# Merge stage: the mLSTM branch by Strassen pairs, the attention branch in plain tiles one pair ahead, the modulation's gate sums moved into the projections

## What is computed

```python
u = rmsnorm(x, norm_pre_w) * (1 + scale) + shift
aq, ak, av, az, mq, mk, mv, mo, mz, mg, ga, gb = split_proj(u, w_in)
y_b = attention(aq, ak, av) * silu(az)                      # (T, 1024)
y_a, C, n, m = mlstm_branch(mq, mk, mv, mo, mz, mg, ...)    # (T, 1024)
merged = sigmoid(ga) * (y_a @ w_proj_a) + sigmoid(gb) * (y_b @ w_proj_b)   # (T, 2048)
out = rmsnorm(merged @ w_out, norm_post_w)
return x + gate * out
```

## Time and profile before

| | |
|---|---|
| median of three runs | 1955.51 us (1955.37 to 1955.70) |
| the profiled execution | 1955.12 us, span 1953.5 us |
| PE busy | 1920.3 us, 98% |
| DVE, ACT, POOL busy | 62%, 34%, 6% |
| mean granted PE clock | 0.998 |
| bytes moved | 274 MB, 140 GB/s in the mean |

### The profile page before, as it was taken

How to read it: one execution, slowest core, us unless ns; L and a number is a source line. 1 busy time by engine, 2 the same in 40 slices (tenths; PEclk the granted TensorE clock), 3 DMA queues, 4 the chain that set the end, 5 groups by cost and what they waited for, 6 DMA issues and landing times.

```text
span 1953.5 us, 31682 instructions
## 1 busy us (share of the span) xinstructions
PE 1920.3 (98%) x12266; PEld 1782.6 (91%) x12266; DVE 1204.0 (62%) x2073; ACT 668.8 (34%) x1017; POOL 113.2 (6%) x201
## 2 busy tenths in 40 slices
PE   6999999999999999999999999999999999999998
PEld 2589999999999999999898999889889999988886
DVE  3368766666666666665766664465557767683224
ACT  4453333333333333332555554233224222242221
POOL 2010000000000000000000000000002000000000
PEclk9999999999999999999999999999999999999999
DMA  9962353333333333334632423355355666633224
GB/s 369 391 197 86 111 164 110 111 112 113 113 113 113 113 113 113 113 113 127 183 109 80 122 75 118 91 150 135 108 130 144 203 203 184 210 116 140 80 76 162
DMA packets 302319, 274.04 MB, mean 140 GB/s; under 512 B 20384, under 2 KB 253608, under 8 KB 300320
## 3 DMA queue, kind: packets, MB, share of 16 engines
q1 hardware_dynamic: 287984, 216.71, 37.9%
q0 software_dynamic: 13952, 56.00, 7.9%
q10 hardware_dynamic: 304, 0.25, 0.0%
HBM read 235.05 MB, written 40.48 MB: 141 GB/s over the span
## 4 chain that ended last, share of the span: by engine, by line
PE 91%; DVE 3%; DMA 3%; ACT 1%; issue 1%; SPq 1%; POOL 0%; DVEq 0%; POOLq 0%; ACTq 0%
PE bank L2060 20%; PE bank L2140 12%; PE bank L2133 12%; PE bank L2134 12%; PE bank L2356 11%; PE bank L2069 10%; PE bank L1973 2%; PE bank L2033 2%; PE bank L2260 2%; PE bank L2249 1%; PE bank L2201 1%; PE bank L2262 1%; PE bank L2178 1%; PE bank L2009 1%; DMA WORK<-in_w_ada_dram 1%
## 5 line engine op out<-in xcount | busy, mean ns | idle before, releaser
L2060 PE MATMUL bank<-XH,WH 128*128 128x320 f32 x1472 | 345.5, 316 | 2.8 <-DVE XL L1847 2.1
L1041 ACT ACTIVATE WH<-RAW 128x1024 fp32r<-128x1024 f32 x195 | 206.7, 1060 | 386.1 <-PE bank L2140 306.2
L2060 PE MATMUL bank<-XL,WH 128*128 128x320 f32 x1472 | 335.1, 309 | 0.0
L1482 DVE TENSOR_TENSOR WL<-RAW,WH 128x1024 fp32r<-128x1024 f32 x195 | 238.3, 1222 | 143.8 <-ACT WH L1041 143.8
L920 ACT ACTIVATE WH<-RAW 128x1024 fp32r<-128x1024 f32 x122 | 129.1, 1059 | 532.3 <-PE bank L2069 407.8
L2060 PEld LDWEIGHTS bank<-XH,WH 128*128 128x128 f32 x1472 | 244.5, 188 | 10.8 <-issue 8.0
L2060 PEld LDWEIGHTS bank<-XL,WH 128*128 128x128 f32 x1472 | 246.2, 188 | 0.0
L2069 PE MATMUL bank<-XH,WL 128*128 128x320 f32 x1472 | 235.9, 310 | 0.0
L2069 PEld LDWEIGHTS bank<-XH,WL 128*128 128x128 f32 x1472 | 220.0, 188 | 4.1 <-issue 3.8
L2134 PE MATMUL bank<-XL,WH 128*128 128x320 f32 x720 | 212.5, 309 | 0.0
L2133 PE MATMUL bank<-XH,WH 128*128 128x320 f32 x720 | 212.5, 309 | 0.0
(11 more groups left out here) (245 smaller groups left out, 2962.9 us busy)
## 6 DMA issues: line engine op xcount, KB each, us to landing
RAW<-in_w_in_dram SPq DMA_DIRECT2D x165, 512.0 KB, 3.8
WORK<-in_w_ada_dram SPq DMA_DIRECT2D x62, 512.0 KB, 5.4
proj_dram<-OUTS POOLq DMA_DIRECT2D x92, 320.0 KB, 2.5
RAW<-in_w_out_dram SPq DMA_DIRECT2D x32, 512.0 KB, 3.9
WORK<-proj_dram SPq DMA_DIRECT2D x16, 640.0 KB, 4.5
WORK<-proj_dram POOLq DMA_DIRECT2D x32, 320.0 KB, 3.3
RAW<-in_w_ada_dram SPq DMA_DIRECT2D x18, 512.0 KB, 9.3
RAW<-in_w_proj_a_dram SPq DMA_DIRECT2D x16, 512.0 KB, 4.7
```

The lines of the kernel that those rows point to most:

```text
L1041: ins = nc.scalar.activation(WH[:, (j + p) % 2, :], pair_raw(j, p), ACT.Copy)
L1482: V.tensor_tensor(WL[:, w, :], pair_raw(j, p), WH[:, w, :].bitcast(F32), ALU.subtract)\
L2060: pe.matmul(banks[n][:, 0:HALF_TOK], wh[:, k, :], x[:, k0 + k, n * HALF_TOK:(n + 1) * HALF_TOK], start=(first and k == 0 and wi == 0), sto ...
```

## The change

- **Merge, attention branch (B):** sixteen plain tiles `b_product(j)`, one half each (48 products). They use blocks 0 to 7 of XH and XL, which now hold attention's result (`shift` of `high_y` and `low_y`). `b_gate(j)` multiplies the banks by the sigmoids in place (MTB). Tiles 0 to 3 come first, then two after each mLSTM pair, one after pairs 5 and 6, none after 7 (`b_tiles`).
- **Merge, mLSTM branch (A):** eight Strassen pairs `a_product(i, p)`, p from 0 to 6, of 12 products each (four blocks of the contraction, three passes). RAW slots 2 and 3 hold the four weight quarters; WH and WL are used in halves (`a_weights`). The four differences of the activations are made once, by POOL (`sub`), and split by ScalarE and VectorE (`ta_high`, `ta_low`). `a_gate(i)` multiplies the pair's two tiles by their sigmoids and adds MTB.
- **The gate's sums** leave the merge: `gada_step(i, j, k)` in the projections' pairs adds one of 16 channel blocks of one of four column groups, two steps a pair (three or four in the last five). POOL loads 256 KB for each, and stores each group to DRAM (`gada_store`). They are read back at the end of the merge (`gs_in`); b_ada is added by two operations on one partition (`gs_bias`).
- The loop of the pairs is over eight pairs, three times; the merge is unrolled. WORK grows to 14500 words, and the scratch for POOL's transfer descriptors is set to 4096 bytes.
- NPW is loaded after the last `a_gate`. At the end of the merge VectorE does four `low_y`, a sum, four `low_y`, and then `lo(2 * T_OUT)`.

The core of the diff (blank lines left out; the waits' changed factors, `2 * n` to `LOOP * n`, and allocations are left out too):

```diff
-T_PAIR, T_L1, T_L2, T_MERGE, T_OUT, T_END = 4, 64, 78, 90, 106, 122
+T_PAIR, T_L1, T_L2, T_MERGE, T_OUT, T_END = 4, 64, 78, 90, 98, 114
 PAIRS = (T_L1 - T_PAIR) // 2
 PAIRS_PLAIN = 27
+LOOP, LOOPS = 8, 3
+GADA_LAST = [4, 3, 3, 3, 3]
...
+LOW_EARLY = 5
...
+def b_tiles(i):
+    return {-1: (0, 1, 2, 3), 5: (14,), 6: (15,), 7: ()}.get(i, (2 * i + 4, 2 * i + 5))
...
+        def a_weights(w, p):
+            return w[:, p % 4 // 2, 512 * (p % 2):512 * (p % 2) + 512]
...
+            def b_half(j):
+                sp.wait_ge(lo_done, 2 * T_MERGE + (j - 1 if j >= 2 else j - 3))
+                sp.dma_start(RAW[:, j % 2, :].rearrange("p (k n) -> p k n", k=8), w_pb_v[:, :, P * j:P * j + P])\
+                    .then_inc(raw_in[j % 2], 16)
+            def a_pieces(i):
+                for n in range(2):
+                    if i:
+                        sp.wait_ge(p_lo, LO_0 + 7 * i)
+                    else:
+                        sp.wait_ge(lo_done, 2 * T_MERGE - 1 + n)
+                    for e in range(2):
+                        sp.dma_start(RAW[:, 2 + n, 512 * e:512 * e + 512].rearrange("p (k n) -> p k n", k=4),
+                                     w_pa_v[:, e:8:2, 2 * P * i + P * n:2 * P * i + P * n + P]).then_inc(raw_in[2 + n], 16)
...
+            b_half(0)
+            b_half(1)
             states_out(M_HEADS - 1)
-            sp.wait_ge(ml_ya, M_HEADS + 1)
-            sp.wait_ge(ml_state_out, 128 * M_HEADS + 16)
-            with sp.Fori(0, 7) as i:
-                for k in range(2):
-                    for x in range(2):
-                        merge_half(i + 1, k, x)
-                        gada_load(i, 2 * k + x)
-            for q in range(4):
-                out_piece(0, q)
-                gada_load(7, q)
-            for q in range(4, 8):
-                out_piece(0, q)
+            a_pieces(0)
+            b_half(2)
+            b_half(3)
+            for i in range(MERGES - 1):
+                for j in b_tiles(i):
+                    b_half(j)
+                a_pieces(i + 1)
...
+            def gada_store(i, m):
+                pool.wait_ge(gada_used, 16 * i + 16 * (m + 1))
+                pool.dma_start(gsum[bass.ds(P * i + P * m, P), :], GACC.rearrange("p v n -> p (v n)")).then_inc(gacc_out, 16)
+                pool.wait_ge(gacc_out, 16 * i + 16 * (m + 1))
+                nc.gpsimd.tensor_tensor(ZERO[:, 7:8], ZERO[:, 0:1], ZERO[:, 0:1], ALU.add).then_inc(gacc_free, 1)
+            def gada_loads(i, m, steps):
+                for k in steps:
+                    if m or k >= 4:
+                        pool.wait_ge(gada_used, 16 * i + (16 * m + k - 3))
+                    pool.dma_start(GAR[:, k % 4, :], w_ada[0, k * P:(k + 1) * P, bass.ds(512 * i + 512 * m + 4096, 512)])\
+                        .then_inc(gada_in[k % 4], 16)
...
+            def gate_b(k):
+                if k:
+                    pool.wait_ge(sig_in[0], 16 * k)
+                pool.dma_start(MTB[k % 2], proj[(RB_GB + 2 * k) * P:(RB_GB + 2 * k + 2) * P, :]
+                               .rearrange("(c p) t -> p c t", p=P)).then_inc(sig_in[0], 16)
...
+            gate_b(0)
+            sub = lambda out, a, b: nc.gpsimd.tensor_tensor(out, a, b, ALU.subtract).then_inc(t_raw, 1)
+            h0, h1 = slice(0, HALF_TOK), slice(HALF_TOK, TOK)
+            sub(TAL[0], YA[:, :, 0, h1], YA[:, :, 0, h0])
+            pool.wait_ge(t_raw, 8 + 1)
+            sub(TAL[1], YA[:, :, 1, h1], TAL[0])
+            gate_b(1)
+            sub(TAL[2], YA[:, :, 1, h1], YA[:, :, 0, h1])
+            pool.wait_ge(t_raw, 8 + 2)
+            sub(TAL[3], YA[:, :, 1, h0], TAL[1])
+            pool.wait_ge(y_lo, KT)
+            pool.wait_ge(t_raw, 8 + 4)
...
+            gate_a(0)
+            gate_a(1)
+            for i in range(MERGES - 2):
+                pool.wait_ge(merged, 2 * i + 2 + 1)
+                gate_b(i + 2)
+                gate_a(i + 2)
+            pool.wait_ge(gacc_out, 16 * 4)
+            pool.wait_ge(p_used, USED_0 + 7 * (MERGES - 1) + PR_S1 + 1)
...
+            pool.wait_ge(merged, KT + 1)
             pool.dma_start(NPW, norm_post_w[0].partition_broadcast(P)).then_inc(gs_in, 16)
...
+            act.wait_ge(yb_done, 10 * KV_HEADS + 1)
             act.wait_ge(w_used, 2 * T_MERGE - 1)
-            high_y(range(8), y_hi)
+            high_y(range(8), y_hi, 8)
...
+            def b_hi(j):
+                act.wait_ge(raw_in[j % 2], RAW_MERGE[j % 2] + 16 * (j // 2 + 1))
+                if j < 4:
+                    act.wait_ge(w_used, 2 * T_MERGE + j - 1)
+                else:
+                    act.wait_ge(p_used, USED_0 + (7 * (j // 2 - 2) + 6 + j % 2 if j < 15 else 7 * 7))
+                nc.scalar.activation(WH[:, j % 2, :], RAW[:, j % 2, :], ACT.Copy).then_inc(hi_done, 1)
+            def a_hi(i, p):
+                if p == PR_A11 or p == PR_A12:
+                    act.wait_ge(raw_in[2], RAW_MERGE[2] + 32 * (i + 1))
+                else:
+                    act.wait_ge(s_ready, READY_0 + 4 * i + {PR_S1: 1, PR_A22: 1, PR_S2: 2, PR_S4: 3, PR_S3: 4}[p])
+                if p >= PR_S3:
+                    act.wait_ge(p_used, USED_0 + 7 * i + p - 3)
+                elif p < PR_S2:
+                    if i < 7:
+                        act.wait_ge(w_used, 2 * T_MERGE + (2 * i + 3))
+                    else:
+                        act.wait_ge(p_used, USED_0 + 7 * 6 + 6)
+                else:
+                    if i == 6:
+                        act.wait_ge(p_used, USED_0 + 7 * 6)
+                    else:
+                        act.wait_ge(w_used, 2 * T_MERGE + min(2 * i + 4, 16))
+                nc.scalar.activation(a_weights(WH, p), a_raw(p), ACT.Copy).then_inc(p_hi, 1)
...
+            b_sigmoid(0)
+            b_hi(2)
+            ta_high(0)
+            ta_high(1)
+            b_sigmoid(1)
+            b_hi(3)
+            ta_high(2)
+            ta_high(3)
+            for i in range(MERGES):
+                a_hi(i, PR_A11)
+                a_hi(i, PR_A12)
+                if 1 <= i < MERGES - 1:
+                    b_sigmoid(i + 1)
+                a_sigmoid(i)
+                a_hi(i, PR_S2)
+                a_hi(i, PR_S1)
+                a_copy(i)
+                for p in (PR_S3, PR_S4, PR_A22):
+                    a_hi(i, p)
+                for j in b_tiles(i):
+                    b_hi(j)
+            act.wait_ge(merged, 8 + 1)
+            act.wait_ge(w_used, 2 * T_OUT)
+            high_y(range(8), m_hi)
             hi(0, 0, 2 * T_OUT)
...
+            def gada_step(i, j, k):
+                m = 0 if j <= LOOP * LOOPS and not (isinstance(i, int) and j > LOOP) else LOOPS
+                dve.wait_ge(gada_in[k % 4], 64 * i + (64 * m + 16 * (k // 4 + 1)))
+                if k == 0:
+                    dve.wait_ge(gacc_free, i + (m + 1))
+                else:
+                    dve.wait_ge(gada_used, 16 * i + (16 * m + k))
+                for v in range(2):
+                    acc = GACC[:, v, :]
+                    col = VC[:, k + 16 * v:k + 16 * v + 1]
+                    if k == 0:
+                        ins = V.tensor_scalar(acc, GAR[:, 0, :], col, None, ALU.mult)
+                    else:
+                        ins = V.scalar_tensor_tensor(acc, GAR[:, k % 4, :], col, acc, ALU.mult, ALU.add)
+                ins.then_inc(gada_used, 1)
...
                     pair_lo(i, j, PR_S3)
+                    gada_step(i, j, steps[1])
                     pair_lo(i, j, PR_S4)
...
+                if q == 4 * L2_TILES * M_HEADS - 2:
+                    low_y(range(LOW_EARLY), y_hi, y_lo, 8)
...
+            def a_gate(i):
+                y = Y[:, 2 * i:2 * i + 2, :]
+                dve.wait_ge(sums, SUMS_0 + 7 * i + 7)
+                dve.wait_ge(sig_done, sigmoid_a(i))
+                chain.link(V.tensor_tensor(y, OUTS[:, :, :], y, ALU.mult))
+                V.tensor_tensor(y, y, MTB[i % 2], ALU.add).then_inc(merged, 2)
+            low_y(range(LOW_EARLY, 8), y_hi, y_lo, 8)
             lo(0, 0, 2 * T_MERGE)
-            low_y(range(3, 8), y_hi, y_lo)
+            low_y(range(8, 12), y_hi, y_lo, 8)
             lo(0, 0, 2 * T_MERGE + 1)
-            low_y(range(8, KT), y_hi, y_lo)
...
-            lo(0, 0, 2 * T_OUT)
-            low_y(range(8), m_hi, m_lo)
-            merge(7, 1)
+            low_y(range(12, KT), y_hi, y_lo, 8)
+            b_gate(0)
+            b_lo(2)
+            ta_low(0, 2)
+            dve.wait_ge(t_raw, 8 + 4)
+            ta_low(1, 2)
+            a_s1(0)
+            b_gate(1)
+            b_lo(3)
+            ta_low(2, 3)
+            ta_low(3, 4)
+            for i in range(MERGES):
+                if i:
+                    a_s1(i)
+                    if i == MERGES - 1:
+                        b_gate(15)
+                    else:
+                        b_gate(2 * i + 2)
+                else:
+                    b_gate(2)
+                a_lo(i, PR_A11)
+                a_s2(i)
+                a_lo(i, PR_A12)
```

(85 more changed lines are left out.)

373 lines of the change are left out of this document (207 added, 166 removed).

## The result

The changed kernel takes 1975.23 us (median; 1974.46 to 1976.47), the kernel before 1955.51. The ratio is 1.0103, with a 95% interval of 1.0089 to 1.0116. The forecast was 1960.8 us, with 1952.5 to 1967.0 as its range: the sign was right, the size was not, and the result lies 8 us beyond the range.

A forecast was written before the change was run, and what follows sets the result against it. TensorE, busy 98% of the span, was taken as the bound. Savings of 14.1 and 1.4 less stalls of 5.9 and 8.8 left 0.8 us saved; 6.1 lost to contention gave about 1960.8 us, range 1952.5 to 1967.

The forecast's parts named there:

- Term 1: Merge: 96 fewer TensorE products at 0.1467 us each, 14.1 us saved.
- Term 2: Start of the merge: attention first, its high parts ready early; 1.4 us saved if VectorE runs freely.
- Term 3: Projections' pairs: the gate's sums fit where VectorE waits, so TensorE has no new wait; 0 us.
- Term 4: Merge, pairs 6 and 7: one attention tile or none between pairs no longer covers TensorE's waits; 5.9 us lost.
- Term 5: Start of the output projection: TensorE waits for the weights' low part, then the bias and gate chain; 8.8 us lost.
- Term 6: Merge's first tiles: GpSimd's four differences and VectorE's low parts exclude each other; 6.1 us lost, between 4.2 and 8.0.
- The clock: Rival: half clock on TensorE after long waits, 1.7 us a stretch, decisive only if GpSimd holds VectorE out; chance 0.06.

The follow-up runs named there:

- e9: e7 with the remaining waits mended by order alone: weights' and gate's splits earlier in the output projection, the last sigmoid earlier in pair 6; 1945.67 us, ratio 0.9950.
- e3: The changed kernel with the first output weights' low part earlier on VectorE and their high part earlier on ScalarE; 1974.27 us, ratio 1.0089.
- e7: The changed kernel with TensorE's loop back at two pairs, the four differences on VectorE, and the edits of e3 and e4; 1955.64 us, ratio 0.9998.
- e4: The changed kernel with a third buffer for the attention branch's last gates, loaded one pair earlier; 1974.72 us, ratio 1.0094.
- e5: The kernel before with TensorE's loop over the projections' pairs turned every eight pairs instead of every two; 1962.82 us, ratio 1.0039.
- e11: The kernel before with TensorE's loop over the projections' pairs turned every six pairs instead of every two; 1970.01 us in a single execution.

## Why the prediction was wrong, step by step

- **Term 1 (14.1 us saved) held.** The product rows of the merge stand 0.147 us apart at full clock, and e9 keeps most of the gain: 14.1 + 1.45 (term 2) less waits that cost 5.6 is 9.9, measured 9.6.
- **Term 2 (1.4 saved) held:** up to the end of the first tile TensorE loses 1.75 us against its pace, before 3.2.
- **Term 3 (0) failed by 7.7 us,** and it is the largest part of the miss: this is the step of the prediction that failed first of all. Its own question was answered rightly: VectorE's sums fit into its gaps, and there is no new TensorE wait in the pairs away from the turns. But the sums needed a body of eight pairs, and the diff gives that body to TensorE too, which has no part in them. I costed what was added to the loop, not its turn; the four packets of instructions that the kernel before loads in 700 us, a sign that its body stays where it is, I had not read.
- **Term 4 (5.9) held:** 1.15, 2.65, 1.30 and 0.41 us of wait, 6.15 with what each costs around it, for 0.85, 3.1 (its own terms add up to 2.9), 1.3 and 0.66.
- **Term 5 (8.8) held in sum,** in part by luck: 6.07 of 6.3 at the start. The 2.5 us of the gate's chain did not appear as a wait, but the half clock behind the first wait cost the same 2.5 us and made TensorE that much later at the gate; e3 and e7, which took the first wait away, show the chain with 3.3 us.
- **Term 6 (6.1 as a middle) was the right mechanism,** with VectorE first, and under-sized: 7.59, where its own price for that order was 4.2. That 6.1 came nearer is luck, as the middle took in an order that didn't occur. A difference takes 2.9 us, not 2.0, 3.5 us for the four, and VectorE's first low part, priced at its free length, was held for some 1.3 more; the prediction had 7.4 for an estimate of 2.8 us from the Trainium skill, "GPSIMD Engine Reference", section "3.1 Elementwise — side-by-side cycle accounting", and the trace bears that out. The lock of the Trainium skill, "SBUF — State Buffer", section "Who interferes with whom", is borne out too (13.66 and 6.53 us); the gating, which has only one operand in SBUF, was not held.
- **The clock had a chance of 0.06 and a condition that was wrong.** I let it decide only if GpSimd held VectorE out throughout, and priced it at 1.7 us. In these runs it follows every wait of TensorE in the merge and the output projection from 3.3 us up, and the pair of 1.15 and 2.65 us (in e4 and e7 also the pair of 1.15 and 1.77); its price was 2.3 to 2.6 each in the changed kernel, some 1.5 behind the shorter pair. Behind tile 3 and pair 6, 4.9 us together, nothing absorbed it.

In sum: -14.1 - 1.45 + 7.7 (turns) + 7.59 (tile 3) + 6.15 (pairs 6 and 7) + 9.1 (6.23 at the output's start, 0.4 later, 2.5 clock) + 4.9 (clock) is 19.9. The span says 20.2. Of the miss of 14.4 us (19.7 for 5.3) the loop's turns are 7.7, the clock behind the merge's waits 4.9 and term 6's size 1.5. The range failed with them: its upper end was built only from bounds of the costs that I had found.

Not settled: why one turn costs 2.6 us and another 4.2 with no half clock in either, and why the half clock follows some turns (one of two in e5, two of three in e11) and none in the trace of the changed kernel, though e3 and e4, with the same pairs, have it at one turn and at both.
